# Merged stage of a hybrid attention step: scoring and gate units, each parted in two, take turns on the tensor engine

## The reference

```python
z = jnp.einsum('bsd,de->bse', h, w_in)
qa, ka, va, ga, qb, kb, vb, gb, ma, mb = jnp.split(z, offs, axis=-1)
# sample rows, branch A: gathered keys of three windows; branch B: 16 pages of 128 keys
scores = jnp.einsum('bthd,btshd->bhts', q, kg) * (d ** -0.5)
out = jnp.einsum('bhts,btshd->bthd', p, vg)
# gates of both branches, for all 1088 rows
ya = (o_a.reshape(b, s, A_WIDTH) * jax.nn.silu(ga.astype(f32))).astype(x.dtype)
yb = (o_b.reshape(b, s, B_WIDTH) * jax.nn.silu(gb.astype(f32))).astype(x.dtype)
m = jax.nn.sigmoid(ma.astype(f32)) * pa + jax.nn.sigmoid(mb.astype(f32)) * pb
```

## Time and profile before

| | |
|---|---|
| runs of the kernel before | 1710.34 us median of 3 (1700.9 to 1713.57) |
| the profiled execution, its own time | 1708.63 us |
| its span in the trace | 1706.8 us |
| TensorE busy over the span | 1632.1 us, 96% |
| VectorE, ScalarE, GpSimd busy | 42%, 35%, 39% |
| packets of TensorE's instruction queue (q8) | 119 |

### The profile page before, as it was taken

The page is one execution under the profiler, slowest core; times in us unless marked ns, Lnnn a source line. Parts: engine busy times, 40 slices in busy tenths (PEclk is TensorE's granted clock), DMA queues, the critical chain, the costliest instruction groups (busy, mean ns, idle before and its releaser), DMA issues.

```text
span 1706.8 us, 37775 instructions
## 1 busy us (share of the span) xinstructions
PE 1632.1 (96%) x14872; PEld 1401.3 (82%) x14872; DVE 719.7 (42%) x1788; ACT 600.1 (35%) x1405; POOL 665.8 (39%) x958
## 2 busy tenths in 40 slices
PE   7999999999999999999999889999899898999998
PEld 5787677878899999999999768778687787878787
DVE  6522576222472222712226534444354432588411
ACT  5422476222362222722226233333333333412300
POOL 5566120567434565445656111221121111566500
PEclk9999999999999999999999999999999999999999
DMA  5164811766417566166433889899889975865422
GB/s 166 53 238 149 268 38 30 238 211 216 145 45 230 196 238 232 51 203 214 138 104 96 282 293 306 277 314 311 270 283 311 316 254 182 285 204 174 147 93 80
DMA packets 184064, 336.30 MB, mean 197 GB/s; under 512 B 29969, under 2 KB 74130, under 8 KB 177746
## 3 DMA queue, kind: packets, MB, share of 16 engines
q1 hardware_dynamic: 143586, 221.68, 39.6%
q10 hardware_dynamic: 40304, 112.22, 19.4%
HBM read 294.05 MB, written 127.07 MB: 247 GB/s over the span
## 4 chain that ended last, share of the span: by engine, by line
PE 86%; issue 3%; DMA 3%; DVE 2%; POOL 2%; ACT 2%; SPq 1%; ACTq 0%; POOLq 0%; DVEq 0%
PE ps L2008 13%; PE ps L2010 13%; PE ps L2009 13%; PE ps L2217 5%; PE ps L2060 5%; PE ps L2061 4%; PE ps L2062 4%; PE ps L2161 4%; PE ps L2107 3%; PE ps L2181 3%; PE ps L2276 3%; PE ps L2259 2%; PE ps L2168 2%; PE ps L2128 2%; PE ps L1977 2%
## 5 line engine op out<-in xcount | busy, mean ns | idle before, releaser
L993 POOL TENSOR_TENSOR w_lo<-raw,w_hi 128x512 fp32r<-128x512 f32 x140 | 181.2, 1300 | 432.3 <-ACT w_hi L1203 417.7
L2008 PE MATMUL ps<-w_hi,hT 128*128 128x512 f32 x824 | 339.8, 412 | 2.1 <-POOL hT L980 1.0
L2010 PE MATMUL ps<-w_hi,hT 128*128 128x512 f32 x824 | 330.2, 401 | 0.0
L2009 PE MATMUL ps<-w_lo,hT 128*128 128x512 f32 x824 | 330.0, 400 | 0.0
L2008 PEld LDWEIGHTS ps<-w_hi,hT 128*128 128x128 f32 x824 | 206.1, 250 | 21.4 <-issue 1.4
L2010 PEld LDWEIGHTS ps<-w_hi,hT 128*128 128x128 f32 x824 | 206.2, 250 | 20.4
L2060 PE MATMUL ps<-w_hi,hT 128*128 128x256 f32 x768 | 221.3, 288 | 1.0 <-issue 0.7
L2009 PEld LDWEIGHTS ps<-w_lo,hT 128*128 128x128 f32 x824 | 206.4, 251 | 18.1
L2061 PE MATMUL ps<-w_lo,hT 128*128 128x256 f32 x768 | 216.5, 282 | 2.9 <-issue 2.9
L2062 PE MATMUL ps<-w_hi,hT 128*128 128x256 f32 x768 | 215.9, 281 | 0.0
L1203 ACT ACTIVATE w_hi<-raw 128x512 fp32r<-128x512 f32 x158 | 99.0, 630 | 215.3 <-DMA raw<-in_w_in 197.9
(11 more groups left out here) (233 smaller groups left out, 2870.3 us busy)
## 6 DMA issues: line engine op xcount, KB each, us to landing
out<-in_cache_a_kv ACTq DMA_DIRECT2D x29, 2040.0 KB, 9.2
k_in<-in_cache_b_kv SPq DMA_DIRECT2D x128, 256.0 KB, 3.6
v_in<-in_cache_b_kv SPq DMA_DIRECT2D x128, 256.0 KB, 6.3
raw<-in_w_in SPq DMA_DIRECT2D x104, 256.0 KB, 4.1
k_in<-in_cache_a_kv SPq DMA_DIRECT2D x104, 256.0 KB, 6.6
v_in<-in_cache_a_kv SPq DMA_DIRECT2D x104, 256.0 KB, 6.7
out<-in_cache_a_kv ACTq DMA_DIRECT2D x7, 2016.0 KB, 8.5
raw<-in_w_in ACTq DMA_DIRECT2D x40, 256.0 KB, 6.1
```

The lines of the kernel that those rows point to most:

```text
L993: pool.tensor_tensor(lo, raw_of(q), hi.bitcast(F32), ALU.subtract).then_inc(lo_done, 1)
L2008: pe.matmul(z, hi, wh, start=first, stop=False)
L2009: pe.matmul(z, hi, wl, start=False, stop=False)
L2010: return pe.matmul(z, lo, wh, start=False, stop=last)
```

## The change

`gate` and `scored` take an argument that says which row tiles, or which of the four parts j, they do; their waits go with the first part and their semaphores with the last. In the loop a slot is `parted` when it has a scoring and exactly one gate unit of two row tiles. In such a slot TensorE does half of the scoring (parts 0 and 1), row tile 0 of the gate unit, the other half (parts 2 and 3), and then, where it stood before, row tile 1. Slots whose unit is the short one stay whole. Only TensorE's program changes; the other engines' instructions are the same and stand in the same order.

```diff
--- before.py
+++ after.py
@@ -2036,14 +2036,19 @@
             def hT_pieces(k, i):
                 return (h[:, k, i * P:(i + 1) * P] for h in hT) if i < NT else (None, None)
 
-            def gate(m):
+            def gate_tiles(m):
+                return range(1 if unit_place(m)[3] == UNITS - 1 else 2)
+
+            def gate(m, tiles=None):
                 _, _, hb, pr = unit_place(m)
-                if m >= 2:
-                    pe.wait_ge(*unit_freed(m - 2))
-                else:
-                    pe.wait_ge(ao, 104)
+                tiles = gate_tiles(m) if tiles is None else tiles
+                if 0 in tiles:
+                    if m >= 2:
+                        pe.wait_ge(*unit_freed(m - 2))
+                    else:
+                        pe.wait_ge(ao, 104)
                 z = bank(6 + m % 2)
-                for t in range(1 if pr == UNITS - 1 else 2):
+                for t in tiles:
                     i = 2 * pr + t
                     for k in range(KC):
                         if pr == 0 and t == 0 and (hb == 0 or hb > 1 and k % 2 == 0):
@@ -2060,7 +2065,8 @@
                         pe.matmul(part, hi, wh, start=k == 0, stop=False)
                         pe.matmul(part, hi, wl, start=False, stop=False)
                         ins = pe.matmul(part, lo, wh, start=False, stop=k == KC - 1)
-                ins.then_inc(z_ready, 1)
+                if tiles[-1] == gate_tiles(m)[-1]:
+                    ins.then_inc(z_ready, 1)
 
             def project(br, i):
                 pe.wait_ge(y_lo[br], i + 1)
@@ -2195,28 +2201,31 @@
             def quadrant(c):
                 return slice(ROW_C * c, ROW_C * c + ROWS_S)
 
-            def scored(x):
+            def scored(x, parts=range(4)):
                 b, n = divmod(x, 4)
-                pe.wait_ge(s_kt, tiles_before(2 * x + 2))
-                if x == 0:
-                    pe.wait_ge(as_, 208)
-                if n == 0:
-                    pe.wait_ge(s_qa, b + 1)
-                    if b:
-                        pe.wait_ge(s_tb, b)
-                if n == 2:
-                    pe.wait_ge(s_ta, b + 1)
-                if n == 1:
-                    pe.wait_ge(s_qb, b + 1)
+                if 0 in parts:
+                    pe.wait_ge(s_kt, tiles_before(2 * x + 2))
+                    if x == 0:
+                        pe.wait_ge(as_, 208)
+                    if n == 0:
+                        pe.wait_ge(s_qa, b + 1)
+                        if b:
+                            pe.wait_ge(s_tb, b)
+                    if n == 2:
+                        pe.wait_ge(s_ta, b + 1)
+                    if n == 1:
+                        pe.wait_ge(s_qb, b + 1)
                 for G, at_, tiles in (((3, 0, 8),), ((2, 0, 4),), ((0, 0, 8),), ((0, 0, 8),))[n]:
                     col, at_ = 256 * (n % 2) + 32 * at_, 8 * (x % 2) + at_
-                    for j in range(4):
+                    for j in parts:
                         for c in range(NC):
                             for i in range(4):
                                 rows, d0 = slice(32 * i, 32 * i + 32), c * P + 32 * j
                                 ins = pe.matmul(bank(i)[quadrant(c), col:col + 32 * tiles], q_rep[rows, G, j, c, :],
                                                 k_tiles[rows, at_:at_ + tiles, d0:d0 + 32],
                                                 start=(j == 0 and n in (0, 2)), stop=(j == 3), skip_group_check=True)
+                if parts[-1] < 3:
+                    return
                 if n == 1:
                     for c in range(NC):
                         ins = pe.matmul(bank(1)[quadrant(c), COLS_R:COLS_R + P], q_new[:, 1, c, :],
@@ -2295,12 +2304,17 @@
                 mine = pieces_at(gg) if gg < N_GROUPS + 5 else []
                 for pb, p in mine[:1]:
                     probs(pb, p)
+                units = gates_at(gg)
+                parted = gg < N_GROUPS and n % 2 and len(units) == 1 and len(gate_tiles(units[0])) == 2
+                if parted:
+                    scored(gg // 2, range(0, 2))
+                    gate(units[0], range(0, 1))
                 if gg < N_GROUPS and n % 2:
-                    scored(gg // 2)
+                    scored(gg // 2, range(2 if parted else 0, 4))
                 if b and n in (1, 5):
                     summed(b - 1, n // 5)
-                for m in gates_at(gg):
-                    gate(m)
+                for m in units:
+                    gate(m, range(1, 2) if parted else None)
                 for pb, p in mine[1:]:
                     probs(pb, p)
                 if n == 2 and b < DEC_B:
```

## The result

The kernel changed took 1713.81 us as the median of 20 runs (1707.89 to 1721.79), the kernel before 1708.84 us of 20 runs on the same chip (1700.04 to 1715.98): a ratio of 1.0032, 95% interval 1.0016 to 1.0048, or +5.0 us where -4.5 was forecast. It is within 1% and inside the range, but on the other side of nothing, and by more than its interval. The profiled execution has a span of 1715.2 us. It reached its first scoring 5.7 us later than that of before did (953.31 against 947.63), ahead of anything that was changed; eleven of the twelve experiments that follow start theirs between 947 and 950 us, so that part is this execution's own.

A forecast was written before the change was run, and what follows sets the result against it. TensorE, 86% of the chain, was taken to bound the kernel, with 29.2 us of instruction stalls. Terms -20.1 - 4.5 + 8.1 + 10.0 + 2.0 gave -4.5 us, so a median of 1706 us, range 1691 to 1722.

The forecast's parts named there:

- Stalls: TensorE's instruction waits in parted scorings: gate matmuls make a packet last longer, removing most of 24.2 us; -20.1 us.
- Changes of form: 27 parted slots switch once more between 32x16 pieces and 128x128 weights and back, 0.3 us each; +8.1 us.
- Late chains: Scorings end 2.86 us later, delaying VectorE's keys and ScalarE's pT that TensorE needs; +10.0 us, bounds 4 and 15.
- The four main places: Slots 8 and 9, 48 and 49: waits for ScalarE's pT or VectorE's keys, 3 to 4 us each.
- the four places behind short units: Slot 27 and three like places (slots 5, 41, 60): ScalarE's piece comes late, 0.8 us each, 3.2 in all.
- Clock: Merged stage: three low-clock stretches behind stalls go, -4.5 us; new waits bring up to two of 1.5, taken as +2.0.
- Nothing else moves: Remaining waits: key loads issue 2.9 us later, but TensorE's key waits are bound by VectorE's order, not a transfer; 0.
- The first: Rival: the gain stays, as chains behind slots 7 and 47 give way and form changes cost 0.15; -18.6 us, chance 0.14.
- The second: Rival: the late scoring decides, chains also short behind four other parted n = 7 slots; +7.1 to +19 us, chance 0.14.
- turning point of 14.5 us: In the second rival: the sum of the late scoring's waits past which the change's forecast turns from gain to loss.
- The third: Rival: stalls only move because a packet's delay decides, so nothing is taken off; +18 us, chance 0.05.
- The prediction's own tests: Profile after: few us of "issue" in parted slots, waits at slots 8, 9, 48, 49, 0.3 us steps, fewer stretches at 0.50.

The follow-up runs named there:

- the shifted kernel: The kernel before with 128 waits on a long-raised semaphore ahead of TensorE's first gate unit, to shift later instructions against the blocks: 1707.03 us, ratio 1.0005.
- a tile ahead: Changed kernel, but in the 27 parted slots row tile 0 precedes the whole, uncut scoring and row tile 1 follows: 1698.21 us, 0.9946 of the kernel before.

## Why the prediction was wrong

**Stalls** (-20.1 forecast). Right: -21.4, of 29.9; the forecast left out the 0.7 of slot 45, which is still there (0.6). In slots that stay whole 3.23, 1.51 and 1.09 us are left, 5.8 where 5.0 was said, and in parted ones 2.6 where 2.1 and 2 were said. Though the longest, 3.23, stands in slot 21 and not in 35 or 55. It had 0.43 us before, and a scoring that stays whole can so stall for longer than it did. The cause, blocks of 256 instructions, is shown by the shifted kernel and the landings of the packets. That the alternation is needed for it was never claimed, and it isn't: a tile ahead does the same.

**Changes of form** (+8.1). 27 x 0.36 = +9.7. The edges were priced right (0.45, measured 0.46). The second half's faster start, for which 0.15 was taken off, gives back 0.10; only pieces of 32 get much of it.

**Late chains** (+10.0). 2.5 for keys, slot 1 aside, and 6.4 for pT, 8.9 in all. The four main places and their sizes were right: 2.68 + 1.22 = 3.9 us at slots 8 and 9, where 3.9 was forecast, and 2.69 + 1.34 = 4.0 at 48 and 49, where 4.2 was, 1.32 of it from before. But the forecast had all 6.8 of new wait there on VectorE's keys: the copy to pT comes first, at slots 8 and 48, and what TensorE waited there it doesn't wait at 9 and 49. Of the four places behind short units, 3.2 us of pT in the forecast, only slot 60 came as said, with the 1.0 us at L2264; at slot 5 the 1.0 us are for keys, at slot 41 it is 0.2 for keys, and at slot 28 none. To leave slots 7 and 47 whole gave 10.4 us, with the clock behind them and some stalls elsewhere.

**Clock** (-4.5 and +2.0). Wrong in sign: 3.4 us more at 0.50 in place of less, which at 1.5 us for each 3.4 is +1.5, not -2.5. The three stretches of 3.4 in parted slots did go, and in slot 35 it is 3.4 us for 6.8. But the two waits of 2.7 us for pT, each with one of 1.2 or 1.3 behind it, brought 6.8 us at the low level each, where the forecast had two short stretches, and the 3.23 us of slot 21 brought 3.4.

**"Nothing else moves"** (0). This is the step that failed. It named the keys' loads 2.9 us later and said that TensorE waits for no transfer; it did not follow SyncE's queue one step further, to the loads of values behind those of keys. These waits are +6.0 us, and every kernel that moves the scorings of n = 1 and 5 with the old order of loads has them; that SyncE's queue is their whole cause stays open. They turn the sign by themselves: -4.5 + 6.0 = +1.5.

The sum of what the runs show is -21.4 + 9.7 + 8.9 + 1.5 + 6.0 = +4.7, against +3.9 in the merged stage of the two traces and +5.0 by the medians. Of the 9.5 us between forecast and result, 6.0 are the values, 4.0 the clock and 1.6 the changes of form, less 1.3 for the stalls and 1.1 for the chains. That is 9.2 for the 9.5, but so close a fit is partly luck: the ratio's own interval is 2.7 us to either side, and a single stall (in slot 21) differs by 2.8 us between the two traces.

**The rivals.** None came. The first fell with slots 8 and 48. The second, the late scoring, had the right place and sign but not its mechanism: behind the other four parted slots of n = 7 only 0.2 us appeared, and its turning point of 14.5 us was reached (2.5 + 6.4 + 6.0 = 14.9) only with a wait it didn't name. The third fell with the stalls.

The prediction's own tests read right for stalls, for the places of the waits for pT and keys (3.9 us at slots 8 and 9 together and 4.0 at 48 and 49, where 3 to 4 was said), and nearly for the step to the gate tile (1078.64 less 1077.24 + 1.13, the last scoring matmul's start: 0.27, where it said 0.3 and more). They failed for the stretches at 0.50. Its bound for waits on VectorE and ScalarE, 15 us, was kept by the new ones (8.9 us); there was none for waits on DMA, which was its blind spot.

## What to carry to other kernels

A stall for instructions can be bought off by putting slower work into the block that precedes it, but whatever that work now delays has to be followed through every in-order queue, SyncE's among them, to the loads behind the one that waits. Try the plain move (a tile ahead) before the alternation: it bought the same stalls without changes of form, and it shifts starts as well as ends, so that chains from one start to the next can keep their length. And look at each place of a repeated change by itself: without 2 slots of 27 the loss became a gain.

## What was not expected of the hardware

- Stalls for instructions stand at a fixed place in the count of instructions (number 193 or 194 of each 256 in the kernel before and the shifted one) and end 1.24 to 1.61 us behind the landing of an instruction packet. With 64 instructions added ahead the places in the scorings moved 64 earlier, and the sum went from 29.9 to 21.6 us.
- A run of 32 scoring matmuls behind another form goes at 0.011 us each, one of 64 or 128 at 0.018. So three alternations cost 0.50 us a slot where one costs 0.36.
- The order in which one queue issues loads of keys and of values moved TensorE's waits for values from 1.5 to 8.5 us in one kernel and from 7.5 to 3.8 in another, with the same transfers.
- The length of a wait did not tell how long the clock stayed low: behind a stall of 3.23 us (slot 21, after) the granted clock was 0.50 for 3.4 us, behind one of 3.14 (slot 35, before) for 6.8, and for 6.8 behind a wait of 2.7 with one of 1.2 in its wake.
